# A two-block transformer kernel on one core: where roots, diagonals and norms of the head-norm units, the scan's steps and the memory rows' norm stand between the weight blocks

## The reference

```
def rms_norm(x, g):
    xf = x.astype(jnp.float32)
    y = xf * lax.rsqrt(jnp.mean(xf * xf, axis=-1, keepdims=True) + RMS_EPS)
    return (y * g.astype(jnp.float32)).astype(x.dtype)

m = rms_norm(mem, norm_mem_g[i])                      # rows of the memory
k = rms_norm(kv[:, :, 0], k_g)                        # heads of the memory's keys
na = neighborhood_attention(rms_norm(heads(nq), na_q_g), rms_norm(heads(nk), na_k_g), heads(nv), rpb)
q = rms_norm(q.reshape(b, s, N_DIFF_HEADS, 2, HEAD_DIM), q_g).transpose(3, 0, 2, 1, 4)
```

## Time and profile before

| | us |
|---|---|
| median of 3 runs | 3913.45 |
| lowest and highest run | 3903.26, 3919.18 |
| the profiled execution, its own time | 3920.65 |
| its span, first to last instruction | 3918.9 |
| PE busy | 3661.4 |
| DVE busy | 2190.3 |
| ACT busy | 1653.7 |
| mean granted clock of TensorE | 0.96 |

### The profile page before, as it was taken

The page is one execution under the profiler, slowest core; times in us unless marked ns, Lnnn a source line. Parts: engine busy times, 40 slices in busy tenths (PEclk is TensorE's granted clock), DMA queues, the critical chain, the costliest instruction groups (busy, mean ns, idle before and its releaser), DMA issues.

```text
span 3918.9 us, 48013 instructions
## 1 busy us (share of the span) xinstructions
PE 3661.4 (93%) x20215; PEld 3142.7 (80%) x20215; DVE 2190.3 (56%) x2825; ACT 1653.7 (42%) x2254; POOL 240.1 (6%) x232
## 2 busy tenths in 40 slices
PE   7878799999997999998999999999998899999999
PEld 7766688998986887877888888888777678888887
DVE  5887624565656545556555555554565565555454
ACT  4334323655643433544444434443333344344343
POOL 3552000000010020000000000000000000000000
PEclk9999879999998999999999999999998899999999
DMA  7324446555554664454656656655332356566664
GB/s 208 97 87 142 138 121 184 146 154 140 140 181 126 188 161 125 136 159 114 187 186 191 184 192 186 190 162 161 108 118 93 122 151 191 187 191 184 193 183 150
DMA packets 859383, 613.09 MB, mean 156 GB/s; under 512 B 10370, under 2 KB 752305, under 8 KB 858144
## 3 DMA queue, kind: packets, MB, share of 16 engines
q1 hardware_dynamic: 857072, 602.21, 52.5%
q0 software_dynamic: 2096, 7.81, 0.8%
HBM read 607.82 MB, written 2.16 MB: 156 GB/s over the span
## 4 chain that ended last, share of the span: by engine, by line
PE 85%; DVE 9%; ACT 2%; POOL 2%; issue 1%; SPq 0%; DMA 0%; DVEq 0%; ACTq 0%
PE acc L901 27%; PE acc L894 26%; PE acc L903 13%; PE acc L913 9%; PE psC L1006 2%; DVE wL L1684 2%; PE psA L975 1%; PE psA L1113 1%; PE psB L961 1%; PE psC L961 1%; DVE xtok L1645 1%; DVE arena L1996 1%; ACT wH L1271 1%; PE psA L867 1%; PE psB L989 1%
## 5 line engine op out<-in xcount | busy, mean ns | idle before, releaser
L1684 DVE TENSOR_TENSOR wL<-ring,wH 128x1024 fp32r<-128x1024 f32 x1128 | 1336.6, 1226 | 1149.8 <-ACT wH L1271 1148.8
L1271 ACT CAST wH<-ring 128x1024 fp32r<-128x1024 f32 x1128 | 1126.3, 1047 | 1297.8 <-PE acc L903 646.9
L901 PE MATMUL acc<-act,wH 128*128 128x512 f32 x4480 | 1595.0, 401 | 0.3
L903 PE MATMUL acc<-act,wL 128*128 128x256 f32 x4480 | 1258.2, 281 | 0.0
L901 PEld LDWEIGHTS acc<-act,wH 128*128 128x128 f32 x4480 | 845.1, 189 | 210.1 <-issue 3.8
L903 PEld LDWEIGHTS acc<-act,wL 128*128 128x128 f32 x4480 | 849.7, 190 | 4.8 <-issue 4.3
L894 PE MATMUL acc<-wH,act 128*128 128x512 f32 x1792 | 579.3, 401 | 26.0 <-DVE act L1676 22.8
L913 PE MATMUL acc<-act,wH 128*128 128x256 f32 x2560 | 481.5, 290 | 18.1 <-DVE wL L1684 18.1
L894 PEld LDWEIGHTS acc<-wH,act 128*128 128x128 f32 x1792 | 344.6, 192 | 106.8 <-issue 21.7
L913 PEld LDWEIGHTS acc<-act,wH 128*128 128x128 f32 x2560 | 407.8, 195 | 23.3 <-issue 10.8
L913 PE MATMUL acc<-act,wL 128*128 128x256 f32 x1280 | 365.2, 285 | 0.0
(11 more groups left out here) (296 smaller groups left out, 2624.6 us busy)
## 6 DMA issues: line engine op xcount, KB each, us to landing
ring<-in_w_ffn_in SPq DMA_DIRECT2D x176, 1024.0 KB, 5.8
ring<-in_w_ffn_out SPq DMA_DIRECT2D x88, 1024.0 KB, 5.1
ring<-in_b_w_in SPq DMA_DIRECT2D x64, 1024.0 KB, 6.3
ring<-in_w_in_ab SPq DMA_DIRECT2D x56, 1024.0 KB, 5.5
ring<-in_w_in_c SPq DMA_DIRECT2D x48, 1024.0 KB, 5.8
ring<-in_kv_w SPq DMA_DIRECT2D x24, 1024.0 KB, 5.6
ring<-in_a_w_in SPq DMA_DIRECT2D x16, 1024.0 KB, 7.3
ring<-in_w_xkv SPq DMA_DIRECT2D x16, 1024.0 KB, 6.0
```

What stands on the lines that cost most here:

```text
L901: pe.matmul(bank.rearrange("p (h t) -> p h t", h=2), high[:, t, :], act2[:, t, :, :], start=t == 0, stop=False)
L903: ins = pe.matmul(bank[:, T:2 * T], low[:, t, :], xH[:, t, :], start=False, stop=t == ph.kt - 1)
L1271: act.copy(wH[:, split_slot, cols], ring[:, slot, cols]).then_inc(h_made, 1)
L1684: dve.tensor_tensor(wL[:, split_slot, cols], ring[:, slot, cols], wH[:, split_slot, cols].bitcast(F32), ALU.subtract).then_inc(l_made, 1)
```

## The change

- `head_roots` (ACT) and `head_norm` (DVE): the `yield` goes behind the root, and behind the diagonal and the norm. The step's blocks follow them. `head_means` on TensorE stays as it was.
- `norm_mem`: the 8 blocks go as 2, 2, 1, 1, 1, 1 over six steps.
- The scan: one item stands before its steps instead of two, and `S5_FILL` has an item at yields 0 to 28 and 30 (before: 0 to 27 and 30). TensorE turns the first widened matrices ahead of the first `s5_z` block, ACT copies them out ahead of that item's cast.
- The memory's row norm on DVE: the statistics of the first 128 rows come three steps earlier, the root's reciprocal and the scaling one step later; ACT's root and scaling one step later. `mean_squares` and `rms_rows` are cut into `row_stats`, `mean_of_squares`, `row_scale` and `scale_rows`, which do the same work.

```diff
--- before.py
+++ after.py
@@ -492,7 +492,9 @@
 
         HALVES = 2 * SSM_TILES
 
-        S5_FILL = [1] * 28 + [0, 0, 1, 0]
+        S5_FILL = [1] * 29 + [0, 1, 0]
+
+        MEM_FILL = [2, 2, 1, 1, 1, 1]
 
         def s5_pair(q):
 
@@ -1083,7 +1085,6 @@
 
             items = join(block_steps(s5_z), *(join(mem_turn(l), block_steps(kv_mem[l][0], TURN_MEM[l]),
                                                    block_steps(kv_mem[l][1])) for l in range(DEPTH)))
-            next(items)
             pe.wait_ge(cols_copied, 3)
             s5_turn(0)
             next(items)
@@ -1100,7 +1101,7 @@
 
 
             alternate(head_means(norm_mem), join(block_steps(kv_cmp[0], TURN_LN1), block_steps(kv_cmp[1])),
-                      [2, 2, 2, 2])
+                      MEM_FILL)
             await_chunks(pe, kv_cmp[1])
             pe.wait_ge(pos_ready, 4)
             for s, (ph, src) in enumerate(zip(cmp_w1, (kcT, vcT))):
@@ -1310,7 +1311,6 @@
                             act.wait_ge(mean_ready, n - 1)
                         act.activation(score[:, n % 2, :], u["x"].rearrange("p a t -> p (a t)"), ACT.Square)\
                             .then_inc(sq_ready, 1)
-                    yield
                     if 0 <= t - 1 < len(part):
                         u = part[t - 1]
                         n = u["n"]
@@ -1321,6 +1321,7 @@
                         act.activation(head_rms[:, n % 2, 0:w], psA[:, n % 2, 0:w], ACT.Sqrt,
                                        bias=consts[:, 0:1], scale=0.5 if u["wide"] else 1.0)\
                             .then_inc(hroot_ready, 1)
+                    yield
 
             def attend(part):
 
@@ -1593,16 +1594,13 @@
         def _(dve):
             chain = Chain(dve, dve_step)
 
-            def mean_squares(call, src, centred):
-
-                if call in STATS_IN_DRAIN:
-                    dve.wait_ge(stats_ready, (D // COLS) * (STATS_IN_DRAIN.index(call) + 1))
-                else:
-                    for m in range(MT):
-                        for k in range(4):
-                            chain.add(dve.bn_stats(stats[:, m, 6 * k:6 * k + 6],
-                                                   src[:, m, k * COLS:(k + 1) * COLS]))
-                    chain.settle()
+            def row_stats(src, m):
+
+                for k in range(4):
+                    chain.add(dve.bn_stats(stats[:, m, 6 * k:6 * k + 6], src[:, m, k * COLS:(k + 1) * COLS]))
+
+            def mean_of_squares(centred):
+
                 for m in range(MT):
                     chain.add(dve.bn_aggr(moments[:, m, :], stats[:, m, :]))
                 chain.settle()
@@ -1614,17 +1612,35 @@
                     chain.add(dve.tensor_tensor(mean_sq[:, :], mean, mean, ALU.mult))
                     chain.settle()
                     dve.tensor_tensor(mean_sq[:, :], mean_sq[:, :], var, ALU.add).then_inc(ms_ready, 1)
+
+            def row_scale(call):
+
                 dve.wait_ge(root_ready, call + 1)
                 dve.reciprocal(rstd[:, :], root[:, :]).then_inc(rstd_ready, 1)
                 dve.wait_ge(rstd_ready, call + 1)
 
-            def rms_rows(call, src):
-
-                mean_squares(call, src, False)
+            def scale_rows(src):
+
                 for k in range(2):
                     cols = slice(k * D // 2, (k + 1) * D // 2)
                     dve.tensor_scalar(hs[:, 0, cols], src[:, 0, cols], rstd[:, 0:1], None, ALU.mult)\
                         .then_inc(scaled[0], 1)
+
+            def mean_squares(call, src, centred):
+
+                if call in STATS_IN_DRAIN:
+                    dve.wait_ge(stats_ready, (D // COLS) * (STATS_IN_DRAIN.index(call) + 1))
+                else:
+                    for m in range(MT):
+                        row_stats(src, m)
+                    chain.settle()
+                mean_of_squares(centred)
+                row_scale(call)
+
+            def rms_rows(call, src):
+
+                mean_squares(call, src, False)
+                scale_rows(src)
 
             def layer_norm(call, l):
                 mean_squares(call, xtok, True)
@@ -1912,6 +1929,8 @@
                 yield
                 scaled_by(3, V(2), 1.0 / TWO_PI, 0.5, ALU.mult, ALU.min)
                 dve.tensor_scalar(V(3), V(3), -0.5, None, ALU.max).then_inc(s5_frac0, 1)
+                dve.wait_ge(mem_landed, 16)
+                row_stats(hs, 0)
                 yield
                 dve.wait_ge(s5_trig0, 2)
                 dve.wait_ge(s5_exp, 2)
@@ -1935,8 +1954,12 @@
                 yield
                 s5_bbar()
                 yield
-                dve.wait_ge(mem_landed, 16)
-                rms_rows(RMS_MEM, hs)
+                row_stats(hs, 1)
+                chain.settle()
+                mean_of_squares(False)
+                yield
+                row_scale(RMS_MEM)
+                scale_rows(hs)
 
             def s5_bbar():
 
```

## The result

The changed kernel takes 3848.9 us (median of 4 runs, 3842.8 to 3850.7) against 3912.3 (4 runs, 3903.3 to 3919.2) of the kernel before: ratio 0.984, 95% interval 0.981 to 0.986. The forecast was 3865, its range 3847 to 3893. The sign held, and so did the named mechanisms; the size was too small: 63 us went by the medians and 70.0 by the two profiled executions (3920.65 and 3850.68), where the sum said 48.3.

What follows compares the result with a forecast made beforehand. TensorE, busy 93% of the span, was taken as the bound. Gains of 22.2 + 6 + 0 + 4.1 + 16.0 = 48.3 us took the profiled 3920.65 us to 3872, less 7.2 for the median: 3865 us, range 3847 to 3893.

Steps and rivals of the forecast that it cites:

- DVE's bound: Scan: upper limit of the gain, 37 us, where DVE would never idle (259 - 221.9).
- Seams' idle: Head norms, after a chunk's last block: TensorE's waits for DVE's diagonal go, 19.6 us mid-stretch plus 2.6 at last filled steps.
- Clock tails: Head norms: slow matmuls at the lower clock after five of thirteen waits for the diagonal go, 6 us, possibly none.
- five tails: Slow first matmuls after five of thirteen head-norm waits; 7.5 us at 1.5 each, taken as 6.
- The sign that it named: Head norms: granted clock at 1.00 after the former waits for the diagonal would show the 6 us right.
- MEM_FILL, 0 (-1 to +2): Memory heads: last two spreads get cover, 1.8 us saved, against a wait of about 1.9 us for the last chunk.
- Memory row norm: Opening: the 4.80 us wait at 85.05 goes, less 0.7 us for earlier statistics: 4.1 us, range 1 to 5.
- Scan: 93 to 352 us: waits gone for low halves 9.4, inputs 6.3, last half 3.3 us, less 3 for turns: 16.0.
- turned tiles: Scan: turns of a half's tiles fall in pairs twice per layer instead of once; charged 3 us (0 to 10).
- Rival 1: Scan: GpSimd becomes the bound, next to nothing of the scan's gain is left, 3881 us; chance 0.18.
- Rivals 2 and 3: Head norms: TensorE waits for low halves instead, 3893 us, chance 0.13; the same past its slack, 3943 us, chance 0.03.
- The slack said to be 2 us: Head norms, one-block steps: low halves end at about 5.4 us, TensorE wants them at over 7: some 2 us spare.

Runs made afterwards that it cites:

- the later scaling: Changed kernel with ACT's half of the memory's rows scaled behind the scan's first item, no longer ahead of the sine tables: 3842.1 us, ratio 0.9809 to the kernel before.

## Why the prediction was right, and where its size was off

- **Where it landed.** The median stands 2 us inside the range's lower end, and that is partly luck: the range was let down to 3847 for a scan nearer DVE's bound, 18 us more than its sum. The scan gave 1 to 2 us more; what filled the room was clock, for which no room was made.
- **Seams' idle, 22.2 us: right.** The 22.2 leave out the last two spreads of the memory heads, 1.8 us, which were priced with MEM_FILL. Like for like, 22.4 us of waits for L1727 became 0.7: 21.7. The mechanism is the one given, with the sharper finding that DVE's half of the edit frees the seam and ACT's only makes it possible.
- **Clock tails, 6 us: too small by 21, the step that failed.** The head-norm stretches gave 51.2 us by the table (16.7 + 10.7 + 23.8) and 52.1 us by the kernel with the yields alone. Waits are 22.1 of them (24.2 less 0.7 and 1.44), so some 27 us are clock, beside an estimated 2 us of hand-overs. 10.5 of them are the compression's matmuls. In the differential heads the two-block stretches took 13.2 to 13.4 us after three of the seams and 11.7 after the change, 5 us together, and the row of spreads at the end 18.5 us before (2808.31 to 2826.77) and 11.2 after (2744.08 to 2755.30): 7.2, of which only 1.0 is the shorter wait. The five tails that the prediction counted were worth some 8 us, near its price. What it put at nothing, without a reason, is the clock behind the last waits of a stretch, in the last spreads and the 128 matmuls of the compression: it priced a tail by the 7 us behind a seam and never looked there. The sign that it named, a clock of 1.00 behind the former seams, came true and could not tell 6 us from 27. And the 6 us of the row at the end are not in every execution: the one with only MEM_FILL changed ran that row at full pace.
- **MEM_FILL, 0 (-1 to +2): right**, 0 alone and some +1 us beside the rest. The 1.44 us before the compression is the wait for the last chunk that was priced at 1.9, against the 1.8 us saved.
- **Memory row norm, 4.1 us: right only as part of the whole.** Alone 0, with the slide 3.7. The reason given for the range's lower end (root, table load and tables ahead of the next cast) was the whole of it alone; in the changed kernel it leaves 0.67 and 2.12 us, which the later scaling takes away.
- **Scan, 16.0 us: right**, 16.8 to 18.4 in the trace and 17.4 by the medians, but the items differ, in the changed kernel. Low halves gave 3.8 of their 9.4 us (of the 10.8 us after, 5.2 are the opening's 3.07 and 2.12), inputs 4.5 of 6.3, the last outputs 1.5 of the 3.3 counted. In their place the turned tiles, charged with 3 us, gave 4.5 (11.8 to 7.3) and GpSimd, taken to stay at 12.8, gave 2.9. That is 17.2 us of waits.
- **Rival 1** (GpSimd): its first product took 3.4 to 3.8 us in 10 of 16 halves before and in as many after, and 1.8 in the others. Slower rows didn't become more. The Trainium skill (GPSIMD Engine Reference, Key points) has the two engines contend when VectorE reads two inputs from SBUF. The traces agree with contention in both kernels; it did not grow. **Rivals 2 and 3**: no wait for a low half at any unit. The slack said to be 2 us is that, but in the two-block steps, not in the one-block steps where it was put.
- **The signs named ahead**: the waits for L1727 are gone but for the last units, the clock is 1.00 behind the former seams, no 4.8 us wait is left near 85 us, and DVE's wait for the sine tables is under 8 us.
- **Stretches without an edit** moved by -1.6 to +2.8 us. The three long ones, with the feed-forward and attention parts, stay inside the 0.3% that the forecast took as a sign against it (1.4 us of 900, 2.8 of 1140, 1.5 of 1090). The -1.6 us are 1.3% of the 126 us behind the scan, which hold neither part; 1.0 of them go where the granted clock stayed low for 6.8 us after and 3.4 before. For the rest see the last section.

## What to carry to other kernels

When a wait of TensorE goes, follow the granted clock to the next long dense stretch, and price what runs in between at both levels: narrow matmuls behind the last wait can be worth more than the wait (here 10.5 us behind 1.8). Read it in more than one execution, for the same code can keep the clock in one and lose it in another. Ask of each wait which instruction is last to come, and free that one; here, moving the other alone changed nothing. Parts that share a queue at one place (here the opening) are not additive: an edit can be worth nothing alone and its full price beside another.

## What the runs showed of the hardware that was not expected

- **The same 128 matmuls, 75 columns wide, take 16.9 or 26.6 to 27.4 us**, as the clock stood or fell before or at their start, and TensorE's unbroken work in them did not raise it: granted clock 0.50 over the whole 26.9 us. Of the fourteen profiled executions here eight had the higher level, all of them with the seams gone; six had the lower one: the kernel before, the four with only MEM_FILL, the scan, the row norm or ACT's yield changed, and the one with waits put back.
- **A short wait costs the clock sometimes, and its length alone doesn't say when.** 0.67 us among narrow means and spreads did, in one execution; 1.34 us there did in four and did not in a fifth, all at the end of the differential heads, and at the end of the retention heads the same wait, with 0.35 us more behind it, did in none of five; 1.4 us in front of joined blocks did not in six of six, 2.26 and 3.59 us there did, once each. That the neighbours matter is likely by this, and not shown.
- **Dense blocks have two paces at a granted clock of 1.00.** The same four half-chunks of the feed-forward part, without a wait, before and then after:

```profile
1866.00:1888.60 22.60, 22.60 (x131) 19.61 (x130) 11.93 (x12) 10.10 (x13) 0.00 (x0) 1.00 0.67 186
```

```profile
1820.50:1842.70 22.20, 22.20 (x131) 19.42 (x130) 11.93 (x12) 10.12 (x12) 0.00 (x0) 1.00 0.69 190
```

A stretch keeps one of the two, 22.62 or 22.20 us, for four to eight such groups in a row, and another execution of the changed kernel had the slower one exactly here. Each such stretch shifts the end by 2 to 4 us; between these two traces they came to -1.7 and +3.4. Much of the scatter of a few us between runs is likely this and the falls of the clock above; what sets the pace is open.
